# A two-strand stage of a hybrid decoder: the RWKV strand cut into 51 steps for a tile instead of 30

## The chip, the cores and the metric

The kernel runs on one core of a Trainium2 chip. The metric is the device time of one execution in microseconds (us); the kernel before takes 6866.55 us in the median of three runs (6847.45 to 6910.30).

The engines are TensorE (PE: matmuls, with its weight loads as PEld), VectorE (DVE), ScalarE (ACT), GpSimd (POOL) and SyncE (SP, which issues the DMAs). Each runs its own list of instructions in the order in which they were written; where one needs what another made, it waits on a semaphore, and all that stands behind it on that engine waits too.

## The reference

Two decoder layers run for a prompt group (1024 tokens) and a sample group (8 x 8 tokens). Each layer has three mixers that read one projection (mLSTM, a sparse attention whose keys an indexer selects, and RWKV-7), then an output projection and a SwiGLU FFN. The change is in the prompt's RWKV mixer, whose reference is a scan over tokens:

```python
def rwkv7_scan(r, decay, k, v, a, b, S0):
    def step(S, inp):
        rt, dt, kt, vt, at, bt = inp
        sa = jnp.einsum('bhvk,bhk->bhv', S, at)
        S = S * dt[:, :, None, :] + sa[..., None] * bt[:, :, None, :] + vt[..., None] * kt[:, :, None, :]
        return S, jnp.einsum('bhvk,bhk->bhv', S, rt)
```

Beside it in the same stage runs the prompt's sparse attention (`prompt_dsa`): index scores of every query block against all keys, the 256 greatest of each row, then softmax attention over those.

## The kernel before, in words

The stages of a layer follow one another: the input projection (with the sample group's index scores), the sample attention beside the prompt's mLSTM, two short stages of the sample group, then **`stage_prompt_mix`** (L2350), then the output projection and the FFN. The loop over the two layers is a loop on the chip. Only `stage_prompt_mix` is touched.

That stage has two **strands** which share no data. `rwkv_strand` (L1592, PSUM banks 0 to 3) takes the prompt in 8 tiles of 128 tokens, with the state `ST` carried from tile to tile. Its chunked form is one long chain of hand-overs: token shift on DVE (L1877), `lora_in` on ACT (L1710 to L1712), transposes on PE (L1779), `lora_T` on ACT, two matmuls (L1785), gate and decay on DVE and ACT, transposes (L1801), `tilde_T` on ACT (L1734), five products on PE (L1767, inside the helper `each`), then five **levels** that build the inverse of a triangular matrix. A level is: PE makes Y = Mn.X, ACT copies it to SBUF (`Yl`, L1741), PE multiplies it with X and XT (two products), and DVE adds them (L1935, L1939); the next level's Y needs these sums. After the levels come `U`, `GT` and `Wv` on ACT, a scan over two chunks of 64 tokens (`sa` on DVE at L1950, the update of `ST` at L1953), and the output, which DVE normalises (L1956 to L1977).

`dsa_strand` (L1989, banks 4 to 7) has four phases: 48 index steps (PE L2085, ACT relu L2151, DVE L2207/L2209); a search of 32 rounds for each row's 256th value, in which DVE counts three of six blocks (L2229), ACT the other three by a sum of signs (L2156), and DVE then moves the candidate (L2219 to L2224, L2305); the selection on DVE (L2236, L2256 to L2263); and the attention, with two steps for each of 64 heads. In its first step, called a here, PE transposes a head's probabilities (L2107, after two short matmuls L2104 that only keep PE busy) and scores another head (L2095), ACT copies the transposed part (L2172) and takes the exponential of a third head (L2163), and DVE adds mask and maximum (L2275). The second step, b, has the rest of the transposes and the product with the values (L2116).

**The order** is fixed when the program is built. Each strand is, for every engine, a generator that yields at the end of each step, and has a list of costs, one for each step. `interleave` (L1570) puts next a step of the strand that is behind in its share of the summed costs; `walk` (L1584) then draws from the generators in that one order on every engine. A step of the one strand may hold nothing for some engine. In the order before, step 10 + 2(j-1) of a tile holds level j's Y on PE, its copy on ACT and the mask on DVE, and the next step the two products on PE and the sums on DVE.

Of the kernel before, what the change touches and what calls it, by code (L numbers as in the profile page):

```python
# [1591 lines left out]
def rwkv_strand(nc, st, l, io, sc, const, bk):  # L1592
# [3 lines left out]
    W, C, NC, levels = P, CHUNK, P // CHUNK, 6  # L1596
    STEPS = 10 + 2 * (levels - 1) + 2 + 2 * NC + 1 + 3
# [107 lines left out]
    def scalar(act):  # L1705
        for t in range(NT):
            at, x = counts(t), xs[t % 2]
            act.wait_ge(y_r, t)
# [15 lines left out]
            yield  # L1724
            act.wait_ge(ce_r, at(ce_r, 1))
# [13 lines left out]
            for j in range(1, levels):  # L1739
                act.wait_ge(Y_p, at(Y_p, j))  # L1740
                act.activation(Y[:, :, :], hw(bk[2]), ACT.Copy).then_inc(Y_r, 1)  # L1741
                yield
                yield
            act.wait_ge(U_p, at(U_p, 1))
# [3 lines left out]
            yield  # L1748
            act.wait_ge(W_p, at(W_p, 2))
            act.activation(Wv[:, :, :], hv(bk[2]), ACT.Copy).then_inc(W_r, 1)  # L1750
            yield
            for k in range(2 * NC):
# [3 lines left out]
            yield  # L1756
            yield
# [6 lines left out]
    def tensor(pe):  # L1764
# [5 lines left out]
        for t in range(NT):  # L1770
# [4 lines left out]

            pe.wait_ge(y_r, t)
# [4 lines left out]
            yield  # L1781
            if t == 0:
                pe.wait_ge(loaded, 16 * N_LOADED)
# [3 lines left out]
            yield  # L1787
            yield
# [3 lines left out]
            yield  # L1792
            yield
# [11 lines left out]

            pe.wait_ge(tT_r, at(tT_r, 4))
            for n, (b_, a_, c_) in enumerate(((1, 1, 0), (2, 0, 1), (3, 2, 0), (0, 1, 3), (1, 2, 3))):
                if n == 4:
                    pe.wait_ge(Mn_r, at(Mn_r, 1))
                each(cols(b_), lambda hh: tT[:, a_, hh, :], lambda hh: tT[:, c_, hh, :]).then_inc(prod, 1)  # L1810
                if n in (1, 3, 4):
                    yield
            for j in range(1, levels):
# [10 lines left out]
                yield  # L1824

# [4 lines left out]
            yield  # L1830
            pe.wait_ge(U_r, at(U_r, 1))
            each(vals(2), lambda hh: XT[:, hh, :], lambda hh: U[:, hh, :]).then_inc(W_p, 1)
            yield
            pe.wait_ge(W_r, at(W_r, 2))
            for c in range(NC):
# [5 lines left out]
                yield  # L1841
                for n in range(2):
                    pe.matmul(bk[3][:, :], keep_awake, awake_row, start=True, stop=True)
# [5 lines left out]
                yield  # L1849
            for hh in range(CH):  # L1850
# [4 lines left out]
            yield  # L1855
            yield
            yield
# [7 lines left out]
    def vector(dve):  # L1865
# [7 lines left out]
        for t in range(NT):  # L1873
# [11 lines left out]
            yield  # L1885
            dve.wait_ge(lora_o, at(lora_o, 1))
            dve.tensor_tensor(zz[:, :], bk[1][:, :], vec["wa0"][:, :], ALU.add).then_inc(z_r, 1)
            yield
# [6 lines left out]
            yield  # L1895
            dve.wait_ge(ld_r, at(ld_r, 1))
# [4 lines left out]
            chain(dve.tensor_tensor(zz[:, 0:CW], kk[:, :], sg[:, 1, :], ALU.mult))  # L1901
            yield
# [6 lines left out]
            yield  # L1909
            dve.wait_ge(prod, at(prod, 1))  # L1910
# [13 lines left out]
            for j in range(1, levels):  # L1924
                if j == 1:
# [19 lines left out]
            yield  # L1945
            dve.wait_ge(W_r, at(W_r, 2))
            for c in range(NC):
                cs = slice(c * C, (c + 1) * C)
                dve.wait_ge(sa_p, at(sa_p, c + 1))
                dve.tensor_tensor(sa[cs, :, :], bk[1][cs, 0:CW].rearrange("p (h v) -> p h v", h=CH), Wv[cs, :, :], ALU.add).then_inc(sa_r, 1)  # L1950
                yield
# [15 lines left out]
            yield  # L1967
            dve.wait_ge(std_r, at(std_r, 1))
# [15 lines left out]
    tile = [4.0, 2.0, 2.0, 2.0, 3.0, 2.0, 2.0, 3.5, 2.5, 2.5] + [2.5, 3.0] * (levels - 1) + [2.5, 2.5] + [2.0, 2.5] * NC + [2.5, 2.0, 2.0, 3.0]  # L1984
# [1546 lines left out]
```

## Time and profile before

| | |
|---|---|
| median of three runs | 6866.55 us (6847.45 to 6910.30) |
| the profiled execution's own time | 6861.67 us |
| its span in the profile | 6859.7 us |
| granted TensorE clock over the span | 0.859 of full |
| PE busy | 5746.4 us, 84% of the span |
| DVE busy | 2910.4 us, 42% |
| ACT busy | 1478.8 us, 22% |
| `stage_prompt_mix`, each of two layers | about 850 us |

Busy time is time in which an engine works on an instruction; a wait for another engine is idle time, and the profile names what ended it. PE's granted clock has two levels, 1.2 and 2.4 GHz; a stretch shown at 0.5 ran at 1.2 GHz throughout.

### The profile page before, as it was taken

To read this page: it belongs to the slowest core of one execution; us is meant where nothing else is said; L and a number is where in the kernel's file an instruction comes from. 1 tells how busy PE (TensorE), PEld (TensorE's weight loads), DVE (VectorE), ACT (ScalarE), POOL (GpSimd) and SP (SyncE) were. 2 spreads that over 40 slices of the span, in tenths; PEclk is the share of its full clock that TensorE was granted. 3 is DMA by queue.
4 is the path that set the end of the run, shared out by engine and by line. 5 is a ranking of instruction groups with operands and counts; after the bars stand their busy time and mean duration, and the time that the engine had idled before them with its cause. 6 is when DMAs were issued, how large, how long until landed. Compare 5 with 4: busy or idle time off the path is not lost. (4 is left out here: it accounts for less than half of the span.)

```text
span 6859.7 us, 63096 instructions
## 1 busy us (share of the span) xinstructions
PE 5746.4 (84%) x22668; PEld 3570.5 (52%) x22746; DVE 2910.4 (42%) x6684; ACT 1478.8 (22%) x2844; POOL 741.9 (11%) x776
## 2 busy tenths in 40 slices
PE   6999687466689899999989996864757888999997
PEld 4544465335567456654455444652446664666543
DVE  3257454457644233330032665533676442343200
ACT  2310122146343111100033001220562431011000
POOL 2400266000000000000033003640000000000000
PEclk9999678575699999999989995775757899999998
DMA  4222333120000231121132313321100003211122
GB/s 149 86 93 79 76 94 98 26 70 8 16 21 5 110 128 54 54 68 58 53 116 79 112 62 86 96 82 39 54 14 11 19 29 124 95 54 57 59 73 92
DMA packets 358058, 462.86 MB, mean 67 GB/s; under 512 B 70259, under 2 KB 261173, under 8 KB 357333
## 3 DMA queue, kind: packets, MB, share of 16 engines
q1 hardware_dynamic: 320932, 358.82, 16.3%
q0 software_dynamic: 36864, 100.71, 4.9%
q8 instruction: 146, 2.39, 0.1%
q14 instruction: 116, 0.94, 0.0%
HBM read 347.87 MB, written 121.69 MB: 68 GB/s over the span
## 5 line engine op out<-in xcount | busy, mean ns | idle before, releaser
L396 PE MATMUL pp<-w_in,nT 128*128 128x512 f32 x2016 | 909.6, 597 | 0.0
L3290 PE MATMUL pm<-w_down,hT 128*128 128x512 f32 x1584 | 685.6, 596 | 24.4 <-DMA hT<-scratch_hT 24.4
L3217 PE MATMUL pg<-nT,wgu 128*128 128x364 f32 (+1 forms) x2112 | 670.4, 471 | 17.5 <-DMA wgu<-in_w_up 17.5
L3217 PE MATMUL pu<-nT,wgu 128*128 128x364 f32 (+1 forms) x2112 | 665.1, 468 | 0.0
L396 PEld LDWEIGHTS pp<-w_in,nT 128*128 128x128 f32 x2016 | 375.7, 191 | 428.3 <-issue 427.6
L3217 PEld LDWEIGHTS pg<-nT,wgu 128*128 128x128 f32 x2112 | 403.8, 191 | 262.2 <-issue 22.2
L3217 PEld LDWEIGHTS pu<-nT,wgu 128*128 128x128 f32 x2112 | 401.3, 190 | 242.3
L3290 PEld LDWEIGHTS pm<-w_down,hT 128*128 128x128 f32 x1584 | 302.8, 191 | 406.7 <-issue 406.7
L2472 POOL DMA_INDIRECT k_sel<-in_cache_k,kv_idx x256 | 246.9, 965 | 1001.5 <-DVE kv_idx L2616 864.6
L3242 DVE TENSOR_SCALAR sig<-exp_neg 128x364 f32<-128x364 f32 x132 | 46.2, 350 | 681.9 <-ACT exp_neg L3228 681.9
L3243 DVE RECIPROCAL exp_neg<-sig 128x364 f32<-128x364 f32 x132 | 319.4, 2420 | 4.5
L3308 DVE TENSOR_TENSOR x_tile<-pm,x_tile 128x512 f32<-128x512 f32 x36 | 24.9, 692 | 685.3 <-PE pm L3290 685.3
L378 POOL DMA_INDIRECT ik<-in_cache_idx_k,idx x256 | 245.3, 958 | 389.6 <-PE pt L431 338.2
L658 DVE TENSOR_SCALAR_CACHE_REDUCE area<-s,cand 128x4160 f32<-128x4160 f32 x62 | 281.9, 4546 | 2.2
L3228 ACT ACTIVATE exp_neg<-pg 128x364 f32<-128x364 f32 x132 | 62.5, 473 | 953.0 <-PE pg L3217 952.8
L2472 POOL DMA_INDIRECT v_sel<-in_cache_v,kv_idx x256 | 245.7, 960 | 152.1 <-PE bank L2536 83.5
L3082 PE MATMUL pm<-w_out,yT 128*128 128x512 f32 x576 | 253.9, 599 | 0.0
L369 POOL MEMSET iq_diag<- 128x1024 f32 x2 | 1.9, 952 | 2285.9 <-issue 2259.1
L640 DVE COPY ikT<-pt 64x512 f32<-64x512 f32 x128 | 87.4, 683 | 375.7 <-PE pt L431 375.7
L518 ACT ACTIVATE proj<-pp 128x512 f32<-128x512 f32 (+1 forms) x144 | 79.5, 552 | 697.1 <-PE pp L396 689.5
L2156 ACT ACTIVATE area<-score,cand 128x768 f32<-128x768 f32 (+2 forms) x192 | 198.0, 1032 | 117.8 <-DVE cand L2305 114.7
L2608 DVE TENSOR_SCALAR_CACHE_REDUCE seen<-bank,c_slots 128x128 f32<-128x128 f32 x256 | 89.6, 350 | 247.7 <-PE bank L2489 242.5
(667 smaller groups left out, 8671.6 us busy)
## 6 DMA issues: line engine op xcount, KB each, us to landing
w_in<-in_w_in SPq DMA_DIRECT2D x14, 2048.0 KB, 9.2
scratch_hT<-hT SPq DMA_DIRECT2D x44, 576.0 KB, 2.8
hT<-scratch_hT SPq DMA_DIRECT2D x18, 1408.0 KB, 7.4
wgu<-in_w_gate SPq DMA_DIRECT2D x44, 512.0 KB, 3.9
wgu<-in_w_up SPq DMA_DIRECT2D x44, 512.0 KB, 5.2
w_down<-in_w_down SPq DMA_DIRECT2D x22, 1024.0 KB
x_all<-scratch_x SPq DMA_DIRECT2D x27, 512.0 KB, 15.2
a_tile<-scratch_pa SPq DMA_DIRECT2D x18, 516.0 KB, 4.7
```

What stands on the lines that cost most here:

```text
L378: pool.indirect_dma_start(ring[J % RING][:, f, :, :].rearrange("p o d -> p (o d)"), None, table, bass.IndirectOffsetOnAxis(ap=idx[:, m, 2 ...
L396: ins = pe.matmul(pp[u % 2][:, 0:cw], nT[:, k, t * P:(t + 1) * P], w[:, k, 0:cw], start=(k == 0), stop=(k == KT - 1))
L518: act.activation(pr[u % PR][:, 0:cw], pp[u % 2][:, 0:cw], ACT.Copy).then_inc(chunk_out, 1)
L640: dve.tensor_copy(kt[J % 2][0:HD, :, :], pt[0][0:HD, :, :]).then_inc(kt_r, 1)
L658: dve.tensor_scalar(hit, s[:, :], value, 0.0, ALU.is_ge, ALU.add, accum_out=cnt[:, k:k + 1]).then_inc(counted, 1)
L2156: act.activation(rank[:, off[i]:off[i] + width(i)], acc[:, off[i]:off[i] + width(i)], ACT.Sign, bias=cand[:, n:n + 1].bitcast(F32), scale= ...
L2472: pool.indirect_dma_start(tiles[n % RING][:, f, :], None, table, bass.IndirectOffsetOnAxis(ap=k_idx[:, n, f:f + 1], axis=0)).then_inc(got[ ...
L2608: chain(dve.tensor_scalar(seen[:, :], p_found[:, f, 0:PAGE], r1_col[:, f:f + 1], 0.0, ALU.is_lt, ALU.add, accum_out=off[:, n, f:f + 1]))
L3082: ins = pe.matmul(pm[t % 2][n][:, :], yT[t % 2][:, k, :], w[:, k, n * 512:(n + 1) * 512], start=(k == 0), stop=(k == KT - 1))
L3217: ins = pe.matmul(bank[:, 0:cw], wb[b][:, which, k, :], nT[:, k, c0:c0 + cw], start=(k == 0), stop=(k == KT - 1))
L3243: chain(dve.reciprocal(e[m % 2][:, 0:cw], sg[m % 2][:, 0:cw]))
L3290: ins = pe.matmul(pm[b][n][:, :], h[b][:, k, :], w[:, k, n * 512:(n + 1) * 512], start=(k == 0), stop=(k == FT - 1))
```

## The change

The RWKV strand has 51 steps for a tile in place of 30. No instruction is added to it or taken out; what changes is between which `yield`s an instruction stands on each engine, and the list of step costs (their sum for a tile goes from 76.5 to 85.9, of which only the shares matter). The consumer of most hand-overs stands one step behind the producer, where it stood in the same step. A level has three steps in place of two: Y on PE; then the copy on ACT, the two products on PE and the mask on DVE; then the sums on DVE. The sparse attention's strand is not touched.

```diff
-    STEPS = 10 + 2 * (levels - 1) + 2 + 2 * NC + 1 + 3
+    STEPS = 19 + 3 * (levels - 1) + 4 + 4 * NC + 5
...
     def scalar(act):
         for t in range(NT):
             at, x = counts(t), xs[t % 2]
+            yield
             act.wait_ge(y_r, t)
             act.wait_ge(shifted, at(shifted, 1))
...
-            for k in range(3):
+            for k in range(4):
                 yield
             for j in range(1, levels):
+                yield
                 act.wait_ge(Y_p, at(Y_p, j))
                 act.activation(Y[:, :, :], hw(bk[2]), ACT.Copy).then_inc(Y_r, 1)
                 yield
                 yield
...
     def tensor(pe):
...
+            yield
+            yield
             pe.wait_ge(y_r, t)
             pe.wait_ge(lora_in, at(lora_in, 1))
...
                 each(cols(0), lambda hh: Y[:, hh, :], lambda hh: XT[:, hh, :]).then_inc(X_p, 1)
                 yield
+                yield
...
     def vector(dve):
...
             for j in range(1, levels):
+                yield
                 if j == 1:
...
             for c in range(NC):
                 cs = slice(c * C, (c + 1) * C)
+                yield
                 dve.wait_ge(sa_p, at(sa_p, c + 1))
                 dve.tensor_tensor(sa[cs, :, :], bk[1][cs, 0:CW].rearrange("p (h v) -> p h v", h=CH), Wv[cs, :, :], ALU.add).then_inc(sa_r, 1)
+                yield
                 yield
...
-    tile = [4.0, 2.0, 2.0, 2.0, 3.0, 2.0, 2.0, 3.5, 2.5, 2.5] + [2.5, 3.0] * (levels - 1) + [2.5, 2.5] + [2.0, 2.5] * NC + [2.5, 2.0, 2.0, 3.0]
+    head = [3.0, 1.5, 1.0, 0.8, 1.5, 0.8, 1.2, 2.0, 1.2, 2.0, 2.0, 1.0, 1.5, 2.0, 1.2, 3.0, 3.0, 2.0, 1.5]
+    scan = [1.5, 0.7, 2.0, 1.0]
+    tile = head + [2.0, 2.5, 1.5] * (levels - 1) + [3.0, 1.5, 1.5, 0.6] + scan * NC + [1.5, 1.2, 1.0, 0.5, 2.5]
```

**On PE, two levels in the sixth tile (tile 5, attention phase).** `X,Mn` is a level's Y, `Yl,XT` and `XT,Yl` its two products; `c_masks,c_ident` to `kT,qT` is a step a, `c_ident,area` followed by `v,area` a step b. Before:

```order
L1767 MATMUL bank_10476<-X,Mn 128x128 x4
L2107 MATMUL bank_10480<-c_ident,area 128x128
L2116 MATMUL bank_10481<-v,area 128x64 x5
L1767 MATMUL bank_10477<-Yl,XT 128x128 x4
L1767 MATMUL bank_10474<-XT,Yl 128x128 x4
L2104 MATMUL bank_10480<-c_masks,c_ident 128x512 x2
L2107 MATMUL bank_10480<-c_ident,area 128x128 x4
L2095 MATMUL bank_10478<-kT,qT 128x512
L2095 MATMUL bank_10479<-kT,qT 128x128
```

With the change:

```order
L1778 MATMUL bank_10476<-X,Mn 128x128 x4
L2139 MATMUL bank_10480<-c_masks,c_ident 128x512 x2
L2142 MATMUL bank_10480<-c_ident,area 128x128 x4
L2130 MATMUL bank_10478<-kT,qT 128x512
L2130 MATMUL bank_10479<-kT,qT 128x128
L1778 MATMUL bank_10477<-Yl,XT 128x128 x4
L1778 MATMUL bank_10474<-XT,Yl 128x128 x4
L2142 MATMUL bank_10480<-c_ident,area 128x128
L2151 MATMUL bank_10481<-v,area 128x64 x5
```

Between Y and the products there now stands a step a where a step b stood, and the step b has gone behind the products.

**On PE, the start of the fifth tile (tile 4), where the attention phase has just begun.** `c_ident,lora_in` are the tile's first transposes. Before:

```order
L2095 MATMUL bank_10478<-kT,qT 128x128
L2095 MATMUL bank_10479<-kT,qT 128x128
L1779 MATMUL bank_10474<-c_ident,lora_in 128x128 x2
L2095 MATMUL bank_10478<-kT,qT 128x128
L2104 MATMUL bank_10480<-c_masks,c_ident 128x512 x10
L2107 MATMUL bank_10480<-c_ident,area 128x128
```

With the change:

```order
L2130 MATMUL bank_10479<-kT,qT 128x128
L2130 MATMUL bank_10478<-kT,qT 128x128
L2139 MATMUL bank_10480<-c_masks,c_ident 128x512 x10
L2142 MATMUL bank_10480<-c_ident,area 128x128
L2130 MATMUL bank_10479<-kT,qT 128x128
L2139 MATMUL bank_10480<-c_masks,c_ident 128x512 x2
L2142 MATMUL bank_10480<-c_ident,area 128x128
L2130 MATMUL bank_10478<-kT,qT 128x128
L1792 MATMUL bank_10474<-c_ident,lora_in 128x128 x2
```

The transposes have gone behind the work of five steps of the attention.

**On DVE, the scan over chunks in the third tile (tile 2, search phase).** `sa<-` and `ST<-` are the strand's, the rest is the search. Before, from the first chunk's update:

```order
L1953 TENSOR_TENSOR ST<-bank_10477,ST 64x256
L1954 TENSOR_TENSOR ST<-ST,chunk_decay 64x256
L2229 TENSOR_SCALAR area,counts<-score,cand 128x640
L2219 SCALAR_TENSOR_TENSOR counts<-sign_sums,half_widths 128x3
L2223 SCALAR_TENSOR_TENSOR keep<-counts,bit_value 128x6
L2224 TENSOR_TENSOR thr<-thr,keep 128x6
L2305 TENSOR_TENSOR cand<-thr,bit 128x6
L2229 TENSOR_SCALAR area,counts<-score,cand 128x384
L1950 TENSOR_TENSOR sa<-bank_10475,Wv 64x256
L2229 TENSOR_SCALAR area,counts<-score,cand 128x512
L1953 TENSOR_TENSOR ST<-bank_10477,ST 64x256
```

With the change:

```order
L1985 TENSOR_TENSOR ST<-bank_10477,ST 64x256
L1986 TENSOR_TENSOR ST<-ST,chunk_decay 64x256
L2264 TENSOR_SCALAR area,counts<-score,cand 128x640
L1981 TENSOR_TENSOR sa<-bank_10475,Wv 64x256
L2254 SCALAR_TENSOR_TENSOR counts<-sign_sums,half_widths 128x3
L2258 SCALAR_TENSOR_TENSOR keep<-counts,bit_value 128x6
L2259 TENSOR_TENSOR thr<-thr,keep 128x6
L2340 TENSOR_TENSOR cand<-thr,bit 128x6
L2264 TENSOR_SCALAR area,counts<-score,cand 128x384
L2264 TENSOR_SCALAR area,counts<-score,cand 128x512
L1985 TENSOR_TENSOR ST<-bank_10477,ST 64x256
```

`sa` stands ahead of the candidate's move, and the move and both counts stand between `sa` and the second update of `ST`.

## Rows read from the trace of the kernel before

**Rows 1.** The page's head, and the two prompt-mix stages: busy time in each.

```profile
span 6859.7 us, 63096 instructions
...
core 0: us, PE busy (x) PEld busy (x) DVE busy (x) ACT busy (x) POOL busy (x), PEclk, DMA share, GB/s
1390.00:2242.00 852.00, 638.25 (x3653) 483.18 (x3692) 507.22 (x1227) 371.49 (x742) 0.00 (x0) 0.76 0.07 24
4792.00:5645.00 853.00, 638.26 (x3653) 483.14 (x3692) 507.51 (x1227) 371.51 (x742) 0.00 (x0) 0.76 0.07 24
```

**Rows 2.** The same view: RWKV tiles 0 to 7 of the first layer.

```profile
1404.66:1511.00 106.34, 89.45 (x447) 54.44 (x448) 73.38 (x120) 50.69 (x106) 0.00 (x0) 0.82 0.11 38
1511.00:1618.91 107.91, 64.94 (x295) 53.56 (x296) 78.11 (x211) 63.75 (x121) 0.00 (x0) 0.55 0.13 42
1618.91:1719.61 100.70, 54.42 (x291) 45.59 (x292) 75.94 (x215) 65.73 (x124) 0.00 (x0) 0.62 0.03 12
1719.61:1819.13 99.52, 59.18 (x295) 49.73 (x296) 82.04 (x157) 23.16 (x42) 0.00 (x0) 0.57 0.03 11
1819.13:1927.29 108.16, 94.89 (x562) 66.03 (x572) 51.58 (x155) 44.95 (x113) 0.00 (x0) 0.88 0.06 19
1927.29:2029.27 101.98, 90.09 (x589) 68.51 (x597) 49.71 (x137) 43.84 (x90) 0.00 (x0) 0.92 0.05 18
2029.27:2145.02 115.75, 103.60 (x601) 79.39 (x610) 50.72 (x131) 43.23 (x82) 0.00 (x0) 0.83 0.04 14
2145.02:2238.60 93.58, 81.68 (x578) 65.94 (x584) 45.27 (x104) 36.14 (x66) 0.00 (x0) 0.94 0.02 5
```

**Rows 3.** The timeline of tile 1, search phase: start, duration, engine, idle before.

```profile
1573.41 2.08 PE L1767 MATMUL bank<-X,Mn 128*128 128x128 f32 x8 [0.78 <-DVE XT L1939]
1576.02 0.57 ACT L1741 ACTIVATE Yl<-bank 128x512 f32<-128x512 f32 x1
1580.47 0.69 DVE L1939 TENSOR_TENSOR XT<-bank,XT 128x512 f32<-128x512 f32 x1 [0.94 <-PE bank L1767]
```

**Rows 4.** DVE's waits in tile 2: total, times, longest.

```profile
DVE ST L1953 <- PE bank L1847: 3.0, 2, 1.5
```

**Rows 5.** DVE's waits in tile 3.

```profile
DVE ST L1953 <- PE bank L1847: 4.5, 2, 2.5
DVE LT L1911 <- PE bank L1767: 3.9, 1, 3.9
```

**Rows 6.** The timeline at the start of tile 4.

```profile
1824.64 1.28 ACT L1712 ACT_TABLE_LOAD   x1
1825.94 0.31 ACT L1712 ACTIVATE lora_in<-pc_tile 128x128 f32<-128x128 f32 x1
1826.39 0.66 PE L1779 MATMUL bank<-c_ident,lora_in 128*128 128x128 f32 x2 [15.21 <-ACT lora_in L1712]
```

**Rows 7.** PE's waits in tile 0, 1404.66 to 1511.00.

```profile
PE bank L1790 <- DVE log_decay L1890: 3.7, 1, 3.7
```

**Rows 8.** The timeline of one level and its neighbours in tile 5.

```profile
1984.30 0.60 PE L2107 MATMUL bank<-c_ident,area 128*128 128x128 f32 x4
1984.94 0.60 ACT L2172 ACTIVATE area<-bank 128x512 f32<-128x512 f32 x1 [3.12 <-PE bank L2107]
1985.42 1.34 PE L2095 MATMUL bank<-kT,qT 64*128 64x512 f32 x4 [0.52 <-DVE mx L2275]
1985.43 0.82 ACT L2163 ACTIVATE area<-area,mx 128x640 f32<-128x640 f32 x1
1986.69 1.16 PE L1767 MATMUL bank<-X,Mn 128*128 128x128 f32 x8
1987.89 0.60 ACT L1741 ACTIVATE Yl<-bank 128x512 f32<-128x512 f32 x1 [1.55 <-PE bank L1767]
```

**Rows 9.** PE's waits in tile 5.

```profile
PE bank L2095 <- DVE mx L2275: 6.0, 8, 1.9
PE bank L1785 <- ACT lora_T L1715: 1.1, 1, 1.1
```

More of the change, by code:

```diff
@@ L1736, in scalar @@
                     yield
-            for k in range(3):
+            for k in range(4):
                 yield
             for j in range(1, levels):
+                yield
                 act.wait_ge(Y_p, at(Y_p, j))
@@ L1743, in scalar @@
                 yield
+            yield
             act.wait_ge(U_p, at(U_p, 1))
@@ L1748, in scalar @@
             yield
+            yield
             act.wait_ge(W_p, at(W_p, 2))
@@ L1751, in scalar @@
             yield
-            for k in range(2 * NC):
+            for k in range(4 * NC - 1):
                 yield
@@ L1755, in scalar @@
             act.activation(y[:, :, :], hv(bk[0]), ACT.Copy).then_inc(y0_r, 1)
-            yield
-            yield
+            for k in range(4):
+                yield
             act.wait_ge(var_r, at(var_r, 1))
@@ L1774, in tensor @@
             V = lambda hh: x[:, 2 * CW + hh * HD:2 * CW + (hh + 1) * HD]
+            yield
+            yield
             pe.wait_ge(y_r, t)
@@ L1781, in tensor @@
             yield
+            yield
             if t == 0:
@@ L1786, in tensor @@
             pe.matmul(bk[2][:, 0:CW], lT[:, 1, :], g2[:, :], start=True, stop=True).then_inc(lora_o, 1)
-            yield
-            yield
+            for k in range(4):
+                yield
             pe.wait_ge(ld_r, at(ld_r, 1))
@@ L1791, in tensor @@
             each(lambda hh: bk[0][0:HD, hh * NC:(hh + 1) * NC], lambda hh: ld[:, hh * HD:(hh + 1) * HD], lambda hh: masks[:, CHUNK_OF, 0:NC]).then_inc(dc_p, 1)
-            yield
-            yield
+            for k in range(4):
+                yield
             for n, b_ in enumerate((1, 2, 3, 0)):
@@ L1804, in tensor @@
                     yield
+            yield
             pe.wait_ge(tT_r, at(tT_r, 4))
@@ L1812, in tensor @@
                     yield
+            yield
             for j in range(1, levels):
@@ L1824, in tensor @@
                 yield
+                yield
             pe.wait_ge(prod_r, at(prod_r, 3))
@@ L1830, in tensor @@
             yield
+            yield
             pe.wait_ge(U_r, at(U_r, 1))
             each(vals(2), lambda hh: XT[:, hh, :], lambda hh: U[:, hh, :]).then_inc(W_p, 1)
+            yield
             yield
@@ L1841, in tensor @@
                 yield
+                yield
                 for n in range(2):
@@ L1849, in tensor @@
                 yield
+                if c < NC - 1:
+                    yield
             for hh in range(CH):
@@ L1854, in tensor @@
             yield
-            yield
-            yield
-            yield
+            for k in range(5):
+                yield
         pe.wait_ge(S_r, NC * NT)
@@ L1884, in vector @@
             dve.tensor_reduce(sm[:, 0, :], h4(tt[:, :]), AX, ALU.add).then_inc(ss_r, 1)
-            yield
+            for k in range(4):
+                yield
             dve.wait_ge(lora_o, at(lora_o, 1))
             dve.tensor_tensor(zz[:, :], bk[1][:, :], vec["wa0"][:, :], ALU.add).then_inc(z_r, 1)
+            yield
             yield
@@ L1895, in vector @@
             yield
+            yield
             dve.wait_ge(ld_r, at(ld_r, 1))
@@ L1901, in vector @@
             chain(dve.tensor_tensor(zz[:, 0:CW], kk[:, :], sg[:, 1, :], ALU.mult))
+            yield
             yield
@@ L1909, in vector @@
             yield
+            for k in range(3):
+                yield
             dve.wait_ge(prod, at(prod, 1))
@@ L1924, in vector @@
             for j in range(1, levels):
+                yield
                 if j == 1:
@@ L1945, in vector @@
             yield
+            yield
+            yield
             dve.wait_ge(W_r, at(W_r, 2))
@@ L1967, in vector @@
             yield
+            yield
             dve.wait_ge(std_r, at(std_r, 1))
```

2 lines of the change are left out of this document (added).

## The prediction

> **What bounds the kernel now.** The windows over the two prompt-mix stages come first, since nothing else is touched: each takes 852 to 853 us of a span of 6859.7, so 1705 us in all, and in each PE is busy 638 us, DVE 507 and ACT 371 [rows 1]. No engine is full over the stage. The windows by RWKV tile say why: they are two kinds of stretch [rows 2]. In tile 0 and tiles 4 to 7, beside the index scores and the attention, PE is busy 89.45 of 106.34, 94.89 of 108.16, 90.09 of 101.98, 103.60 of 115.75 and 81.68 of 93.58 us: PE sets the pace there, and leaves 16.9 + 13.3 + 11.9 + 12.2 + 11.9 = 66.1 us idle a layer. In tiles 1 to 3, beside the search and the selection, PE is busy 55 to 65 of about 100 us, and its clock is 0.55 to 0.62. In tiles 1 and 2 the RWKV chain sets the pace, in tile 3 DVE nearly does (82.04 of 99.52).
>
> A level in the search phase shows the chain [rows 3]: Y starts on PE at 1573.41 and takes 2.08, its copy starts on ACT at 1576.02, 0.53 after Y's end, because ACT is still with a sign of the search; the sums end on DVE at 1580.47 + 0.69 = 1581.16. So a level takes 7.75 us, of which 0.53 is a wait behind the other strand. A level in the attention phase shows PE's side [rows 8]: PE's only wait is 0.52, ahead of a score matmul, for DVE, which came late to the mask because it had stood at the sums.
>
> **The change, part by part.** The same instructions run, so busy time stays but for ACT's table loads; only waits can move. What the change promises is that a consumer no longer stands idle at a hand-over. That pays where the idle engine sets the pace. All terms are for one layer.
>
> *Tiles 1 and 2.* The order shows nearly the same neighbours on DVE at the first update of `ST`, and at the second the candidate's move and two counts in place of one count. DVE waits 3.0 us at the two updates in tile 2 [rows 4]. I take half, 1.5 us in each tile, so 3; bounds 0 (the chain is as long, and the count only fills the gap) and 3.0 each. In the levels ACT's copy stands behind a sign of the search in both orders, so I cost them at nothing: PE's and DVE's work between is the same chain, and its 7.75 us would hide the search's own operations. If a sign that waits for its candidate comes between, that cover is gone (a rival below).
>
> *Tile 3.* DVE nearly sets the pace and waits 4.5 us for `ST` and 3.9 for the first product [rows 5]; with selection steps ahead of both in its queue these 8.4 us become work. I take 6, since the chain itself is then later by part of it; bounds 0 and 8.4.
>
> *Start of tile 4.* PE waits 15.21 us for `lora_in`, until 1826.39, and the attention's steps are queued behind [rows 6]; the tile began at 1819.13 [rows 2], so 7.3 us of that wait lie in it. The order puts five steps of attention ahead of the transposes. I take 5 us; bounds 0 and 7.3. At the other starts of a tile the same hand-over goes a step or two later, but the last steps of a tile on DVE (normalisation, then the shift) stand ahead of the attention's mask, which PE's score needs: the wait at the transposes turns into one at the score. Nothing there.
>
> *Tile 0.* PE waits 3.7 us for `log_decay` [rows 7], behind which index matmuls are queued; these now come first. I take 2; bounds 0 and 3.7.
>
> *Tiles 4 to 7, levels.* This is where the change costs. Before, Y is followed on PE by a step b, and ACT copies Y at once (Y starts 1986.69, the copy 1987.89). With the change the copy on ACT comes behind a step of the attention, and the products stand in the same step as the copy: this one hand-over has lost its step. Behind Y come, by the order, the transposes (0.60), whose copy on ACT takes 0.60, then the exponential, 0.82, then Yl, 0.60: 2.6 us with no hand-over latency. PE has in that time the transposes, 0.60, and the score matmuls, 1.27 from their start to Y's (1985.42 to 1986.69) [rows 8], 1.9 in all. So PE waits about 0.75, and about as long (0.60 and the hand-overs) where no step lies between. Against that DVE reaches the mask in time, and the 0.52 goes. With the hand-overs 0.9 against 0.5: +0.4 x 20 levels = 8 us more. Bounds: 0.5 less and 1.5 more per level.
>
> *Tiles 4 to 7, the rest.* PE waits 6.0 us for masks in tile 5, of which five levels at 0.52 explain 2.6; of the other 3.4 I let the longest, 1.9, stay, since it fits the score behind the normalisation, and 1.5 goes; of the 1.1 at `lora_T` [rows 9] a part. I take 1.8 per tile, 7 us; bounds 0 and 3.4 + 1.1 = 4.5 each.
>
> *ACT's table loads.* In the order, the stage holds 48 in place of 46. A load is 1.28 us, and the activation behind it starts 1.30 after the load's start [rows 6]. ACT is idle for more than half of most tiles, so I take half of 2 x 1.3, 1 us; bounds 0 and 2.6. The Trainium skill (page "ScalarE: Activation LUTs", section "What ACT_TABLE_LOAD costs") counts a drain of 1.38 us beside the 1283 ns, 2.66 us for every switch. By that the two would be 5.3 us a layer at most, an estimate from that page, and the sum 2 to 3 us worse. The row has no such gap.
>
> SP's loads and stores of a tile stand at the same step, and the tile boundaries fall on the same attention steps in both orders; POOL has nothing here.
>
> **Sum.** 3 + 6 + 5 + 2 - 8 + 7 - 1 = 14 us gained a layer, 28 in all. The profiled execution took 6861.67, 4.9 below the median of the runs, 6866.55; so 6834 against its own time, and against the median 6838.5. I say 6838, 0.4% less. The three runs before lie 0.9% apart, so about 1% (69 us) is what can be told from no change.
>
> **The rivals.**
>
> *The waits were worth more (chance 0.34).* PE's clock is the second price: a PE-bound window of t us at granted clock c loses about t x (1 - c): 106.34 x 0.18 + 108.16 x 0.12 + 101.98 x 0.08 + 115.75 x 0.17 + 93.58 x 0.06 = 65.6 us a layer [rows 2]. It is lowest in the tiles whose starts leave PE idle. If PE works through the starts and its gaps close in part, a third of those 65.6 and of the 66.1 idle come back, 44, with the 14 above 58 a layer, 116 in all: 6750. For it speaks tile 4's start, against it that the mask then holds PE at the later ones. The Trainium skill (page "TensorE: Matmul & The Clock Gate", section "What's actually happening") says that the throttled clock is the default and activity releases it; by that rule fewer gaps return clock, and the granted clock here does sit lowest where PE is idlest, 0.55 in tile 1 against 0.94 in tile 7.
>
> *Yl becomes the bound (chance 0.18), slower.* Its place is ACT's queue between Y and the products. If PE waits out copy, exponential and Yl, 0.60 + 0.82 + 0.60 = 2.0 us, on the 25 levels of tiles 0 and 4 to 7 instead of 0.52, that is 37 us; if in the 15 levels of tiles 1 to 3 the copy waits 2.0 in place of 0.53 because a sign before it waits for a candidate, 22 more. My sum without its level term gains 22 (14 + 8): 59 - 22 = 37 a layer, 74 in all: 6941. It decides from 14 / 40, some 0.35 us a level above my charge; beyond 1% slower at (14 + 34) / 40 = 1.2. For it speaks that ACT and PE share that step, against it that ACT is idle more than half the time.
>
> *The order is in effect the same (within the likeliest case, 0.48).* The strands are matched by shares, tile starts stay, and ACT's neighbours in the levels hardly change: 6867. My forecast and this one can't be told apart.
>
> **Chances and range.** 0.48 for within 1% (6798 to 6935), centred at 6838; 0.34 for the clock's case, mostly faster by over 1%; 0.18 for Yl's, mostly slower by over 1%, but part of it falls within. Faster 0.34, same 0.51, slower 0.15. The best bounds of my terms together are 6 + 8.4 + 7.3 + 3.7 + 10 + 18 = 53 us gained a layer, 6760; the worst 30 + 2.6 = 33 lost, 6932. To leave out no more than 2 in 10 the range reaches to the clock's case at the lower end (6750) and halfway from the edge of 1% to Yl's at the upper: 6745 to 6920.
>
> **What the profile after would show.** The two stages would take about 838 us in place of 852. ACT waits at `area L2156` and `Yl` should hardly change in tiles 1 and 2; DVE's waits at `ST` and `LT` in tile 3 should be gone; PE's wait at `lora_in` should end sooner against tile 4's shift; PE should wait for `Yl` by 0.8 to 1.0 us in most levels of tiles 4 to 7, where [rows 8] show none, and less at `mx`. I am wrong if the clock in tiles 4 to 7 moves by more than 0.05, if PE's wait for `Yl` passes 1.5 us, or if tiles 1 and 2 change by over 5 us each.

## The result: 0.95% slower, and the profile after

The change made the kernel slower: 6927.65 us (median of 15 runs, 6880.76 to 6954.57) against 6856.24 (15 runs, 6830.83 to 6910.3), a ratio of 1.0095 (95%: 1.0074 to 1.0116), 65 us. I had forecast 6838.

The profiled execution took 6880.76, the lowest of the 15. Its stages show the loss none the less: 860 and 868 us from the first shift to the last copy, against 833.5 and 833.4. The rest of that execution, with the same instructions, happened to be some 40 us shorter than in the profile of before, so the spans are no measure here and I compare stages, each of them one execution. First the page's head and the windows over the two stages, then RWKV tiles 0 to 7 of the first layer (the columns are those of [rows 1]):

```profile
span 6878.7 us, 63192 instructions
...
1375.00:2253.00 878.00, 666.08 (x3692) 497.51 (x3692) 506.82 (x1225) 373.20 (x744) 0.00 (x0) 0.74 0.07 23
4780.00:5665.00 885.00, 681.05 (x3692) 507.26 (x3692) 507.00 (x1225) 372.85 (x744) 0.00 (x0) 0.73 0.07 23
...
1389.79:1497.27 107.48, 89.10 (x452) 52.36 (x452) 73.17 (x120) 51.70 (x106) 0.00 (x0) 0.87 0.10 35
1497.27:1600.80 103.53, 60.29 (x293) 51.23 (x292) 77.97 (x211) 63.61 (x121) 0.00 (x0) 0.57 0.13 43
1600.80:1701.81 101.01, 59.26 (x292) 49.35 (x292) 76.20 (x216) 65.28 (x124) 0.00 (x0) 0.55 0.03 10
1701.81:1801.86 100.05, 57.31 (x297) 48.01 (x297) 82.13 (x158) 24.55 (x43) 0.00 (x0) 0.59 0.04 12
1801.86:1911.86 110.00, 98.44 (x587) 67.34 (x588) 51.68 (x154) 43.82 (x115) 0.00 (x0) 0.92 0.06 19
1911.86:2024.09 112.23, 101.30 (x582) 75.75 (x581) 50.00 (x137) 41.33 (x86) 0.00 (x0) 0.80 0.05 16
2024.09:2136.27 112.18, 99.88 (x611) 74.65 (x611) 50.27 (x131) 45.70 (x84) 0.00 (x0) 0.88 0.05 15
2136.27:2250.30 114.03, 100.49 (x585) 78.82 (x584) 45.40 (x104) 37.21 (x66) 0.00 (x0) 0.77 0.01 4
```

Against [rows 2] tile 1 is 4.4 us shorter, tile 5 is 10.3 and tile 7 20.5 longer. Tiles 0 to 3 together are 2 to 3 us shorter in each layer, so the whole loss lies in tiles 4 to 7. DVE's and ACT's busy time is what it was, to 2 us [rows 1]; PE's is 28 and 43 us higher in the two layers for the same instructions (some 3 us of it only because the trace of before lacks the records of 39 matmuls a layer), and the column before the last two tells why: PEclk fell from 0.92 to 0.80 in tile 5, from 0.94 to 0.77 in tile 7. I count a window's **half-speed loss** as t x (1 - c), as in the prediction. In tiles 4 to 7 it was 46 us a layer before and is 71 and 83 now; PE's idle time there was 48.8 (45.5 in e14 below, where these tiles are the same and no matmul is missing) and is 47.9 and 45.2 us. So of the 29 and 37 us that these tiles grew by, 24 and 36 are half-speed loss, and the waiting in all hardly changed.

Of PE's two waits that the prediction speaks of, the one for `Yl` grew by 10.4 us a layer. The one for the mask comes 7 times in place of 18, but is no smaller in sum: what is left of it stands around the starts of tiles, with 4.5 us at tile 4's. The waits of PE in tiles 4 to 7 (total, times, longest), before and then after:

```profile
PE bank L2095 <- DVE mx L2275: 12.8, 18, 1.9
PE bank L1767 <- ACT Yl L1741: 0.7, 1, 0.7
```

```profile
PE bank L2130 <- DVE mx L2310: 13.7, 7, 4.5
PE bank L1778 <- ACT Yl L1750: 11.1, 16, 1.2
```

And one level in tile 5 after, the counterpart of [rows 8]:

```profile
1968.28 1.11 PE L1778 MATMUL bank<-X,Mn 128*128 128x128 f32 x8
...
1970.19 1.34 PE L2130 MATMUL bank<-kT,qT 64*128 64x512 f32 x4
1970.29 0.60 ACT L2207 ACTIVATE area<-bank 128x512 f32<-128x512 f32 x1 [2.60 <-PE bank L2142]
1970.79 0.82 ACT L2198 ACTIVATE area<-area,mx 128x640 f32<-128x640 f32 x1
...
1971.60 0.58 ACT L1750 ACTIVATE Yl<-bank 128x512 f32<-128x512 f32 x1
1972.24 1.16 PE L1778 MATMUL bank<-Yl,XT 128*128 128x128 f32 x8 [0.71 <-ACT Yl L1750]
```

Y is done by 1969.39, but its copy stands behind the attention's exponential until 1971.60; PE has run out of work and waits 0.71. The score matmul no longer waits. That is the wait and nearly the size that I had predicted (0.75 to 0.9). What it was worth is another matter.

What a drop of the clock looks like: in tile 5 the transposes of `lora_in` and then the cumulative sum wait, PE starts the latter after 1.57 us of idleness, and for the 27 us behind it runs at half speed (1.2 GHz) while it is full (the clock had been back at full for 3.4 us):

```profile
1928.89 1.22 PE L1804 MATMUL bank<-log_decay,c_masks 128*128 128x256 f32 x2 [1.57 <-DVE log_decay L1913]
```

```profile
1925.07:1928.48 3.41, 2.26 (x11) 1.26 (x10) 0.00 (x0) 3.18 (x6) 0.00 (x0) 1.00 0.00 0
...
1928.80:1956.00 27.20, 27.11 (x106) 20.29 (x107) 12.48 (x38) 9.92 (x20) 0.00 (x0) 0.50 0.00 1
```

Nearly 14 us are lost there behind a wait of 1.6. The Trainium skill (page "TensorE: Matmul & The Clock Gate", section "A second HAM failure mode: psum-queue depth-cycling") says that in another kernel short but frequent idle times between groups of matmuls let the clock swing between its two levels. This trace agrees: in tiles 4 to 7 of the first layer there are eight stretches at half speed, and each begins at or within about 1 us of the end of a wait of 1.3 to 3.3 us.

### The profile page after: what moved, and what is told of

It reads as the page before. It is cut to its first block and busy times, and to the rows that moved or that the text cites. A ratio compares the mean times of both kernels' runs of the same rounds, so it can differ in the third digit from the quotient of the medians.

```text
span 6878.7 us, 63192 instructions
## 1 busy us (share of the span) xinstructions
PE 5782.3 (84%) x22746; PEld 3590.2 (52%) x22746; DVE 2910.7 (42%) x6684; ACT 1481.5 (22%) x2848; POOL 739.3 (11%) x776
## 5 line engine op out<-in xcount | busy, mean ns | idle before, releaser
L2130 PE MATMUL bank<-kT,qT 64*128 64x512 f32 (+3 forms) x384 | 186.1, 599 | 27.2 <-DVE mx L2310 27.2
## 6 DMA issues: line engine op xcount, KB each, us to landing
x_all<-scratch_x SPq DMA_DIRECT2D x27, 512.0 KB, 15.2
```

Source lines behind the costliest of these rows:

```text
L2130: pe.matmul(bk[n % 2][:, 0:cw], qT[e, kv // 2 * 2 + g, i * P:(i + 1) * P], kT[e, kv // 2, c0:c0 + cw], start=True, stop=True).then_inc(s_p, 1)
```

## The experiments

Each was timed in five rounds against the kernel before on the same chip; ratios are to that kernel, with 95% intervals. e9 to e12 ran on another chip, on which the kernel before takes 6973.72 us, so only their ratios count. In the kernels that move steps, the step numbers stand in tables (ACT_AT, PE_AT, DVE_AT: at which step of a tile a piece of work is issued) in place of the yields; with the numbers of before or of the change they issue what those two kernels issue, in the same order. Only the entries that matter are shown.

**The three parts and the costs, each alone in the kernel before.**

```diff
 e1  -PE_AT  = {'lora_p': 0, 'lora_o': 1, 'cum': 3, 'tT': (5, 6), 'prod': (7, 8, 9), ...}
     +PE_AT  = {'lora_p': 2, 'lora_o': 4, 'cum': 8, 'tT': (12, 13), 'prod': (15, 16, 17), ...}
 e2  -level: Y 0, Yl 0, products 1, sums 1 of 2 steps
     +level: Y 0, Yl 1, products 1, sums 2 of 3 steps
 e3  -from U: PE sa (2, 4), S (3, 5), y 6; ACT y0 6, std 8; DVE out 9 of 10 steps
     +from U: PE sa (4, 8), S (6, 10), y 11; ACT y0 11, std 15; DVE out 16 of 17 steps
 e4  -tile = [4.0, 2.0, 2.0, 2.0, 3.0, ...] + [2.5, 3.0] * 5 + [2.5, 2.5] + ... + [2.5, 2.0, 2.0, 3.0]
     +tile = [5.21, 2.60, 2.60, 2.60, 3.91, ...] + [2.73, 3.27] * 5 + [3.3, 3.3] + ... + [1.76, 1.41, 1.41, 2.12]
```

> The kernel before with the change's step numbers in the head of a tile alone (from the shift to the products: 19 steps in place of 10); the costs of the head add up to what they did, so that levels and tail stand where they stood. Theory A (clock): PE's work thins out where a head hand-over waits among more steps, its clock drops to half and stays there for 20 us and more while PE is full; the profile after the change had such stretches behind the heads of tiles 5, 6 and 7. Then the head alone carries half or more of the loss: +30 to +50 us in all, with the half-speed time of tiles 4 to 7 up by 10 to 20 us a layer and PE's idle time unchanged. Theory B (the Yl hand-over has no step left between Y and the products): 0, within 10 us of before. Theory C (only the places changed, by the new costs): 0.

> The kernel before with the change's step numbers in the five levels alone (three steps each in place of two, the copy of Yl in the step of the products), costs of a level adding up to what they did. Theory A (clock in heads and tails): 0 to +10 us in all. Theory B (Yl's hand-over): most of the loss, +40 to +70 us, with PE waiting for Yl by 1 us or more in most levels of tiles 4 to 7. Theory C (places): 0.

> The kernel before with the change's step numbers from U to the normalisation alone (17 steps in place of 10), costs of the three parts of it adding up to what they did. Theory A (clock): the profile after the change had a half-speed stretch of 30 us at the end of tile 7, behind a gap in the tail: +10 to +30 us in all. Theory B (Yl): 0. Theory C (places): 0.

> The kernel before with all its own 30 steps, each hand-over where it was; only the costs are scaled so that head, levels, U and W, scan and end have the shares of a tile that they have in the change (head 0.38 in place of 0.33, end 0.08 in place of 0.12). It tells what the new costs alone do by shifting the RWKV steps against the search and the attention. Theory C (places): most of the loss, +40 to +70 us. Theories A and B: within 15 us of before.

Measured: e1 0.9993 (0.9972 to 1.0013), e2 1.0087 (1.0056 to 1.0118), e3 1.0059 (1.0037 to 1.0082), e4 1.0136 (1.0106 to 1.0165). So my first theory, that the head's scattered hand-overs cost the clock, fell: the head alone costs nothing. The levels alone cost nearly what the whole change costs. And the costs alone, with each hand-over in its old step, cost more than the whole; the four sum to 2.75% against 0.95%. The tail (40 us) and the costs (93) came out above what I had expected of them (10 to 30 and 40 to 70). The parts do not add: where the chain's waits fall against the attention matters as much as how many there are.

**The copy of Yl.** e7 is the changed kernel with this alone undone, e10 the kernel before with this alone done; e13 and e14 split e10 by tile, e15 undoes it in the changed kernel in tiles 4 to 7 alone.

```diff
 e7   -ACT_AT = {..., 'Yl': {1: 20, 2: 23, 3: 26, 4: 29, 5: 32}, ...}
      +ACT_AT = {..., 'Yl': {1: 19, 2: 22, 3: 25, 4: 28, 5: 31}, ...}
 e10  -ACT_AT = {..., 'Yl': {1: 10, 2: 12, 3: 14, 4: 16, 5: 18}, ...}
      +ACT_AT = {..., 'Yl': {1: 11, 2: 13, 3: 15, 4: 17, 5: 19}, ...}
 e13  -                yield from go("Yl", j)
      +                yield from go("Yl moved" if t >= 4 else "Yl", j)
 e14  the same with t < 4; e15 with t >= 4 and e7's numbers, in the changed kernel
```

> The changed kernel with one thing undone: ACT copies Yl in the step of Y, as before, and so a step ahead of the products. Theory B (the Yl hand-over lost its step): most of the loss comes back, 6860 to 6890. Theory A (clock, by the places of the long waits at a tile's head): within 20 us of the changed kernel, 6910 to 6950.

> The kernel before with one hand-over moved: ACT copies Yl in the step of the products instead of the step of Y, in all five levels of all tiles; all else as before. Theory B (this hand-over is what cost): slower by 40 to 80 us, 6900 to 6940, with PE waiting for Yl in most levels of tiles 4 to 7. If it matters only together with the longer levels: within 15 us of before. My price in the prediction, 0.4 us a level on 20 levels and 2 layers, would give +16 us.

> The kernel before with the copy of Yl a step later, in the products' step, in tiles 4 to 7 alone. Theory B1 (both kinds of tile pay, the attention's through PE's clock): the profile with all tiles moved was 20 us a layer longer in tiles 4 to 7, with PE's idle time there unchanged and the half-speed loss 17 us up; so +30 to +45 us in all. By the prediction's own price (0.4 us a level): +16 us. Theory B2 (the search's tiles pay alone, the rest is chance of phase): within 10 us of before.

> The kernel before with the copy of Yl a step later in tiles 0 to 3 alone. With all tiles moved, PE waited 39 us for Yl in tiles 1 and 2 (10 levels) in place of 14, and ACT 84 us for the search's candidate in place of 57, and tiles 0 to 3 were 23 us longer a layer. Theories B1 and B2: +40 to +60 us. If the copy's place in the attention's tiles were all that counts: within 10 us of before.

> The changed kernel with the copy of Yl back in Y's step in tiles 4 to 7 alone. All tiles moved back gave -62 us against the changed kernel; by the two profiles 14 and 23 us a layer of that lay in tiles 4 to 7, 5 to 6 in tiles 1 to 3. Theory B1: -35 to -50 us against the changed kernel, a ratio to before of 1.002 to 1.004. Theory B2 (the search's tiles): -12 us or less, 1.008.

Measured: e7 1.0009 (0.9990 to 1.0027): nine tenths of the loss is back. e10 1.0134 (1.0108 to 1.0159), 91 us, more than the whole change and than the 40 to 80 us that I had expected. e13 1.0078 (1.0047 to 1.0109) and e14 1.0063 (1.0039 to 1.0087) add up to it. e15 came to 1.0057 (1.0037 to 1.0076), which neither theory had: it brings back 0.38 of the 0.95%, and e7, with the copy early in the other tiles too, another 0.48.

That 0.48% isn't all lost in the search's tiles, though the copy differs in tiles 0 to 3 alone. e7 and e15 issue the same instructions in the same order in tiles 4 to 7, yet there e15 takes 449.4 us a layer and e7 433.5. Nearly all of it is tile 4, the first behind the search, in both layers. Tile 4 of e7, then of e15, then a stretch within the latter:

```profile
1800.29:1907.95 107.66, 98.35 (x588) 67.21 (x588) 51.69 (x155) 44.19 (x115) 0.00 (x0) 0.92 0.06 19
```

```profile
1812.50:1934.22 121.72, 113.14 (x588) 76.83 (x588) 52.16 (x154) 44.15 (x115) 0.00 (x0) 0.79 0.05 17
...
1849.17:1876.48 27.31, 27.31 (x100) 20.07 (x99) 9.49 (x23) 4.94 (x16) 0.00 (x0) 0.50 0.02 8
```

In e15 the clock falls behind a wait of 0.93 us and stays at half for 27 us in which PE never idles. So part of what the copy changes in tiles 0 to 3 shows as clock in tile 4. How much of it is due to the copy stays open: the changed kernel, with the copy late in all tiles, takes 110 and 113 us in its tile 4.

The search's tiles themselves pay by plain waiting. A level of tile 1 in e14 (ACT's signs L2164, the copy L1753, the products L1774):

```profile
1566.33 0.94 ACT L2164 ACTIVATE area<-score,cand 128x768 f32<-128x768 f32 x1 [4.93 <-DVE cand L2313]
...
1567.26 1.03 ACT L2164 ACTIVATE area<-score,cand 128x896 f32<-128x896 f32 x1
...
1568.29 1.13 ACT L2164 ACTIVATE area<-score,cand 128x1024 f32<-128x1024 f32 x1
...
1569.42 0.58 ACT L1753 ACTIVATE Yl<-bank 128x512 f32<-128x512 f32 x1
...
1570.05 2.08 PE L1774 MATMUL bank<-Yl,XT 128*128 128x128 f32 x8 [3.21 <-ACT Yl L1753]
```

The copy stands behind three signs, and these behind a candidate that DVE makes only behind the chain's own sums: PE waits 3.2 us in place of a copy behind one sign [rows 3]. Over tiles 1 and 2 (PE's wait for Yl, ACT's for the candidate), in the kernel before and in e14:

```profile
PE bank L1767 <- ACT Yl L1741: 13.8, 10, 2.9
```

```profile
ACT area L2156 <- DVE cand L2305: 56.8, 26, 6.2
```

```profile
PE bank L1774 <- ACT Yl L1753: 37.4, 10, 6.4
```

```profile
ACT area L2164 <- DVE cand L2313: 84.7, 26, 6.5
```

Tiles 1 and 2 took 236.2 us in e14 against 208.6. In the changed kernel, whose steps fall otherwise against the search, it is 15.2 us of waiting for Yl, against 8.8 in e7 and the 13.8 of before.

The attention's tiles pay by the clock. Tiles 4 to 7 in e13, and in the second layer of e14, where they are as in the kernel before (the trace of before lacks 35 of its 2360 matmuls there, this one none):

```profile
1817.69:2257.21 439.52, 390.41 (x2360) 291.14 (x2360) 196.89 (x522) 167.16 (x350) 0.00 (x0) 0.85 0.04 13
```

```profile
5273.26:5692.37 419.11, 373.63 (x2360) 279.81 (x2360) 196.91 (x523) 168.19 (x350) 0.00 (x0) 0.89 0.04 14
```

20.4 us longer, of which 3.6 is idle time (49.1 against 45.5) and 16.8 the same matmuls at a lower clock. In e13 PE waits 7.1 us for Yl there (8 times) in place of 0.7, and 10.6 for the mask in place of 12.8.

**Is the clock a cause, or does it only go with the waits?** e5 and e6 fill four waits of tiles 4 to 7 with matmuls that compute nothing, in the changed kernel and in the kernel before; e9 fills the wait for Yl; e17 and e18 take away and double those that the kernel before has ahead of each head's transposes.

```diff
 e5, e6  +            awake(3, 6, t)     # 6, 4, 6, 4 of them, if t >= 4
          pe.wait_ge(lora_in, at(lora_in, 1))
          ... likewise ahead of lora_T, ld_r and U_r
 e9      +                if t >= 4 and j > 1:
         +                    for k in range(3):
         +                        pe.matmul(bk[3][:, :], keep_awake, awake_row, start=True, stop=True)
                          pe.wait_ge(Y_r, at(Y_r, j))
 e17     -    WAKE, AWAKE = 10, 2
         +    WAKE, AWAKE = 10, 0
 e18     +    WAKE, AWAKE = 10, 4
```

> The changed kernel with matmuls that compute nothing (the 128x512 of the kernel's own keep_awake) put on PE ahead of four of its waits in tiles 4 to 7: 6 ahead of lora_in, 4 ahead of lora_T, 6 ahead of log_decay, 4 ahead of U. They add 20 matmuls a tile of about 0.21 us each at full clock, 17 us of PE work a layer, most of it in time that PE waited. Theory A (each wait of 1 us and more on PE can drop its clock to half for 7 to 30 us, in which a full PE loses half): 4 of the 8 half-speed stretches of tiles 4 to 7 in layer 1 begin behind these waits, and go; the half-speed loss there falls from 70 to 83 us towards 40, and the time falls by 20 to 80 us against the changed kernel, to 6850 to 6910. Theory B (Yl) and a theory in which the clock only follows the idle time: nothing comes back, and the added work costs 0 to 30 us, 6930 to 6960.

> The kernel before with the same filling at the same four waits. Theory A: before has fewer half-speed stretches behind these waits (2 of 6 in tiles 4 to 7 of layer 1), so it gains less than the changed kernel does: -20 to +15 us against before. Where the clock only follows the idle time: +0 to +30 us.

> The changed kernel with 3 matmuls that compute nothing (128x512, some 0.21 us each at full clock) on PE ahead of its wait for Yl in levels 2 to 5 of tiles 4 to 7: 16 levels a layer, 10 us of PE work, and the small waits there are 4 us a layer longer in sum than with the copy a step earlier. Theory B through the clock (the small waits for Yl keep PE's activity low, and its clock low for longer): the half-speed loss in tiles 4 to 7 falls to 50 to 60 us a layer and the time to 6880 to 6910. Theory B by plain waiting: the matmuls cost more than the waits that they fill, 6930 to 6950.

> The kernel before without the two matmuls that compute nothing ahead of each head's transposes in the attention (AWAKE = 0 in place of 2). It leaves out 126 such matmuls a layer; at some 0.2 us each that is 25 us of PE work a layer, 50 in all. Theory A (PE's idle stretches cost through the clock): PE is idle where they stood, the half-speed loss in tiles 4 to 7 rises from 47 us a layer by 30 or more, and the time rises in spite of less work, +20 to +150 us. If the clock were no cause but only went with slow runs: -30 to -50 us.

> The kernel before with four of them in place of two: 25 us more of PE work a layer, 50 in all. Theory A: part of it falls into PE's waits, and the half-speed loss in tiles 4 to 7 falls from 47 us a layer to 20 to 35; the time -20 to +30 us. Without an effect of the clock: +40 to +50 us.

Measured: e17 1.0066 (1.0050 to 1.0083), 39 us slower with 252 matmuls less; e18 1.0019 (1.0002 to 1.0037), 12 us slower with 252 more, whose PE work at full clock is some 53 us (an estimate: 0.21 us each, the distance of their starts in the trace). The half-speed loss of tiles 4 to 7 went from 46 us a layer to 83 in e17 and to 32 in e18, as the theory had it. So the clock is a cause and does not only go with the waits. Tiles 4 to 7 of e17:

```profile
1812.76:2244.83 432.07, 378.89 (x2234) 290.25 (x2234) 197.09 (x522) 167.10 (x350) 0.00 (x0) 0.81 0.04 14
```

With 126 matmuls fewer PE is 5.3 us longer busy than in the row of e14, at 0.81 in place of 0.89.

The same code also shows it by itself. Two layers of one execution run the same orders: tile 6 in the two layers of e14, and tile 4 in those of e9:

```profile
2046.18:2167.48 121.30, 111.67 (x601) 85.18 (x601) 50.73 (x132) 41.44 (x79) 0.00 (x0) 0.75 0.04 14
5483.42:5599.19 115.77, 104.45 (x609) 79.36 (x610) 50.73 (x132) 43.24 (x82) 0.00 (x0) 0.83 0.04 14
```

```profile
1895.38:2019.26 123.88, 115.51 (x600) 77.73 (x600) 52.15 (x154) 43.83 (x115) 0.00 (x0) 0.80 0.05 17
...
5406.43:5516.83 110.40, 100.72 (x599) 68.24 (x600) 51.68 (x154) 43.82 (x115) 0.00 (x0) 0.92 0.05 19
```

13.5 us between two passes over the same instructions, with half-speed losses of 25 and 9. In tile 6 of e14's first layer the clock falls behind a wait of 0.6 us and stays at half for 34 us.

Filling is no sure remedy. e6 gained, 0.9977 (0.9961 to 0.9993), as theory A allowed. e5 came to 1.0075 (1.0055 to 1.0095), against 1.0095 for the change: its 6911 is just above the range that theory A gave, and the half-speed loss of tiles 4 to 7 stayed at 69 in layer 1 (it was 71) and fell to 66 from 83 in layer 2. e9 came to 1.0148 (1.0119 to 1.0177): PE's waits for Yl fell to 2.6 and 3.2 us in tiles 4 to 7, but the loss there is 90 and 76. The waits of the levels do not lower the clock by themselves, then, or three matmuls cost as much as they save; the idea that these small waits keep the clock down is not borne out.

**Can the rest be mended?**

```diff
 e8   the changed kernel, its costs scaled to before's shares:
      -head 32.2, levels 30.0, U and W 6.6, scan 10.4, end 6.7
      +head 25.5, levels 27.5, U and W 5.0, scan 9.0, end 9.5
 e11  e8 and e7 together
 e16  -level: Y 0, Yl 1, products 1, sums 2 of 3 steps
      +level: Y 0, Yl 1, products 2, sums 3 of 4 steps
 e12  e1 and e6 together
```

> The changed kernel's 51 steps with costs scaled so that head, levels, U and W, scan and end keep the shares that they had before (the opposite of the scaling that cost the kernel before 1.4%). Theory C (shares shift the strand against the attention, and that is the loss): the time comes back to before's, 6840 to 6880. If the finer steps themselves cost: it stays at 6910 to 6950. The sum of the three parts made alone (0, +57 and +42 us) would give 6955.

> The changed kernel with both things undone that each brought time back: Yl copied in Y's step (-62 us against the changed kernel) and the costs of head, levels, U and W, scan and end at before's shares (-34 us). If the two act apart: 6832. If both only remove the same half-speed stretches of PE: 6865, no better than the first alone. If the head's, scan's and end's finer steps cost on their own as the tail alone did (+42): 6900.

> The changed kernel with four steps a level: Y, then its copy, then the products, then the sums, each in a step of its own, at the same cost of a level in all. So there are 56 steps a tile. If the missing step between copy and products is the fault: the time of the version with the early copy or better, a ratio to before of 0.997 to 1.003. If a later copy costs wherever it stands (it comes behind the search's sign and the attention's exponential in ACT's queue all the same): 1.008 to 1.015.

> A version that may beat both: the finer head alone (-5 us against before, within its interval) together with the filling of four waits on PE in tiles 4 to 7 (-16 us against before). If the two act apart: 6835 to 6840, 0.3% below before. If the head's finer steps already remove the waits that the filling fills: 6845 to 6860, since 17 us of matmuls a layer are then pure work.

Measured: e8 1.0045 (1.0031 to 1.0059), half of the loss back with the copy as late as in the change. e11 1.0093 (1.0067 to 1.0118): two mends that help alone do not help together, and none of my three expectations had that. With e8's costs the early copy makes the kernel slower, not faster. Its tiles 4 to 7 have the least idle time of all but e6 and e12 (32 us a layer) and the greatest half-speed loss (107). e16 1.0124 (1.0102 to 1.0147): with a step of its own between copy and products it is slower still, so giving the hand-over a step of its own is no remedy. e12 0.9970 (0.9956 to 0.9984) and e6 are below both kernels; their intervals overlap, so the finer head adds nothing that is shown. e12 has the least loss in tiles 4 to 7 (29 us, idle 31).

**All of them together** (a layer's stage and its tiles 4 to 7, means of the two layers of the one execution profiled; loss and idle are the half-speed loss and PE's idle time in tiles 4 to 7, where PE sets the pace):

| kernel | ratio | stage us | tiles 4 to 7 us | loss us | PE idle us |
|---|---|---|---|---|---|
| e12 | 0.9970 | 821.2 | 412.7 | 29 | 31 |
| e6 | 0.9977 | 828.8 | 415.5 | 33 | 32 |
| e1 | 0.9993 | 823.1 | 413.5 | 44 | 41 |
| before | 1 | 833.5 | 419.1 | 46 | 49 |
| e7 | 1.0009 | 840.2 | 433.5 | 56 | 47 |
| e18 | 1.0019 | 836.8 | 427.6 | 32 | 39 |
| e8 | 1.0045 | 851.8 | 440.8 | 67 | 43 |
| e15 | 1.0057 | 865.0 | 449.4 | 78 | 43 |
| e3 | 1.0059 | 855.5 | 443.4 | 75 | 49 |
| e14 | 1.0063 | 860.9 | 422.5 | 53 | 43 |
| e17 | 1.0066 | 845.2 | 432.0 | 83 | 53 |
| e5 | 1.0075 | 869.3 | 459.5 | 68 | 43 |
| e13 | 1.0078 | 851.7 | 439.4 | 65 | 49 |
| e2 | 1.0087 | 857.3 | 438.2 | 57 | 58 |
| e11 | 1.0093 | 880.0 | 466.4 | 107 | 32 |
| change | 1.0095 | 864.1 | 452.3 | 77 | 47 |
| e16 | 1.0124 | 885.2 | 470.2 | 97 | 46 |
| e10 | 1.0134 | 877.1 | 439.2 | 65 | 49 |
| e4 | 1.0136 | 883.7 | 460.4 | 83 | 64 |
| e9 | 1.0148 | 878.6 | 463.9 | 83 | 42 |

e5, e6, e9, e12 and e18 have more matmuls than the others, e17 fewer. Among the fourteen with the same matmuls, tiles 4 to 7 grow longer as the half-speed loss grows, from 413.5 us at 44 to 470.2 at 97. PE's idle time does not follow: e11 has the least of the fourteen and the most loss.

## Why the prediction was wrong

**The step that failed: the levels of tiles 4 to 7, priced as waiting alone.** The term was 8 us a layer, from 18 more at `Yl` and 10 less at the mask. The place was right (the copy behind the exponential). PE's waits for Yl grew by 10.4 us a layer (0.7 to 11.1), and those for the mask did not shrink. But waiting is not what these tiles lost by: made by itself in the kernel before (e13), the late copy costs 0.78% there, 53 us, 27 a layer, and in the profile 16.8 of 20.4 us are the same matmuls at a lower clock. In the changed kernel, undoing it there (e15) brings 0.38%, some 13 us a layer. I had used t x (1 - c) from [rows 2] only in a rival that gains, never against the change.

**The gains failed by as much.** I had forecast 14 us gained a layer, and 33 were lost, 47 apart. By e7 the late copy costs 30 a layer where I charged 8, which is 22 of the 47. Without its level term my sum had 22 us a layer to gain; e7, which is the change without the late copy, loses 3 (1.0009): that is the other 25.

*Tiles 1 to 3* did gain. In e7 they are 10 us a layer shorter than before, where I had 9, and 3.5 in the changed kernel. DVE's waits in tile 3 [rows 5] fell from 4.5 and 3.9 to 2.1 at `ST` and none at `LT`, yet the tile takes 100.05 us in place of 99.52. Tiles 1 and 2 are 4 and 6 us shorter in the two layers. My "I cost them at nothing" for their levels was wrong all the same: I took the copy to stand behind one sign in both orders, and a step later it can stand behind two or three and behind the candidate they wait for (e14). With the copy back (e7) the two tiles are 6.5 and 3.4 us shorter still.

*Tile 0* was to gain 2 and is 1.1 and 0.7 us longer. *At tile 4's start* the wait at `lora_in` [rows 6] gave way to one for the mask:

```profile
1801.81 0.79 PE L2130 MATMUL bank<-kT,qT 64*128 64x128 f32 x2 [4.50 <-DVE mx L2310]
```

It turned there as I had said for the later tiles only, and tile 4 is 1.8 us longer.

*Tiles 4 to 7* took the gains back. In e7 they are 14 us longer than before, 10 of it half-speed loss, and most of that is tile 7:

```profile
2121.08:2233.83 112.75, 99.89 (x585) 78.36 (x584) 44.98 (x104) 37.34 (x66) 0.00 (x0) 0.77 0.01 3
```

That is the clock and nearly the length of tile 7 in the changed kernel (114.03), so the greatest growth of a single tile is not the copy's. With the costs alone (e4) tile 7 takes 124 us at 0.72, with the tail alone (e3) 102 and 105, with the levels alone (e2) 96 at 0.92. So it goes with the costs more than with the levels; no run takes it further apart.

**Slips in the working.** The upper bound of the range does not follow from its own words: halfway between 6935 and 6941 is 6938, not 6920, and the result, 6927.65, lies between the two. Had it been counted inside, that would have been luck: the direction and the price of the clock were wrong all the same. The clock does not "sit lowest where PE is idlest": PE is idler in tile 2 (54.42 busy of 100.70), at 0.62, than in tile 1, at 0.55. And the tile boundaries do not fall on the same steps of the attention: tile 4 holds 588 weight loads in place of 572, tile 5 581 in place of 597.

**Tests.** The clock in tiles 5 and 7 moved by 0.12 and 0.17, beyond the 0.05 that I had named. PE's wait for Yl in tiles 4 to 7 stayed under 1.5 us (longest 1.2), and tiles 1 and 2 changed by under 5 us each. The two stages, which I had put at 14 us less each, took 27 and 35 us more.

**The rivals.** Slower by 74 us through Yl was the right rival with half the right reason; the 65 us lie between it and my upper bound, 6920. Its waits came to 0.7 us a level, not 2.0. That the clock would take back what the head, scan and tail gain, I had left out. What stays open: which waits drop the clock, and for how long. e11 with the least waiting of the unfilled kernels has the most loss, and the wait of 1.57 us in tile 5 is followed at once by 27 us at half speed in the changed kernel and by no drop in e7. I can show that the loss follows the clock, and that moving the copy back removes nine tenths of it; not by which single wait it came, nor why with e8's costs the early copy costs time (e11).

## To carry to other kernels

In a kernel that interleaves two strands by shares, try each copy that another engine waits for as early in its queue as it can stand: a step later puts it behind the other strand's work, and behind what that waits for. Here that was worth 0.9 to 1.3% with two tables of costs, and cost 0.5% with a third. Where an engine's clock falls behind short waits, price a new wait by the half-speed time behind it too (in e13 16.8 us of it for 3.6 us of idle time), on both signs of the forecast, and take the sum of such terms as uncertain by as much. And a table of costs alone moved the time by 1.4% one way (e4) and 0.5% the other (e8); try two or three scalings before judging a finer schedule.

## What was not expected of the hardware

A PE that was 100% busy stayed at 1.2 GHz for 27 us behind a wait of 1.6 us, and in e15 behind one of 0.93. Identical work in two layers of one execution differed by 13.5 us in one tile through the clock alone. Leaving out 252 matmuls that compute nothing made the kernel 39 us slower. And one chip took 6974 us for the kernel for which others took 6850 to 6861.
